# The rests of u chunks 7, 8 and 15 to 24: from GpSimd to VectorE, between its routing operations

## The reference

```python
def peer(xn, w_q, sub_keys, u, v):                 # xn: 256 x 1024
    q = (xt @ w_q).reshape(t, PEER_HEADS, 2, PEER_HALF)
    sc = jnp.einsum("thpc,hpnc->thpn", q, sub_keys).astype(jnp.float32)
    top_s, top_i = lax.top_k(sc, PEER_TOPK)        # 16 of 128 keys, for 8 heads and 2 halves
    cand_s = (top_s[:, :, 0, :, None] + top_s[:, :, 1, None, :]).reshape(...)   # 16 x 16 sums
    best_s, best_pos = lax.top_k(cand_s, PEER_TOPK)
    idx = jnp.take_along_axis(cand_i, best_pos, axis=-1)
    gate = jax.nn.softmax(best_s, axis=-1)
    ...
    act = jnp.einsum("cd,ced->ce", xc, u[ic]).astype(jnp.float32)
    hid = (jax.nn.gelu(act, approximate=False) * gc).astype(xc.dtype)
    return jnp.einsum("ce,ced->cd", hid, v[ic])
```

## Time and profile before

| | |
|---|---|
| three runs, us | 1731.01, 1735.48, 1737.76 |
| their median | 1735.48 us |
| the profiled execution's own time | 1731.88 us |
| its span (first to last instruction) | 1729.9 us |
| busy share of the span | PE 93%, PEld 75%, DVE 74%, ACT 46%, POOL 23% |
| mean granted clock of TensorE | 0.976 of full speed |

### The profile page before, as it was taken

The page is one execution under the profiler, slowest core; times in us unless marked ns, Lnnn a source line. Parts: engine busy times, 40 slices in busy tenths (PEclk is TensorE's granted clock), DMA queues, the critical chain, the costliest instruction groups (busy, mean ns, idle before and its releaser), DMA issues. The chain is left out here.

```text
span 1729.9 us, 24818 instructions
## 1 busy us (share of the span) xinstructions
PE 1610.1 (93%) x9420; PEld 1303.3 (75%) x9420; DVE 1278.4 (74%) x1565; ACT 798.1 (46%) x1033; POOL 392.7 (23%) x184
## 2 busy tenths in 40 slices
PE   7995899899999996999988999999999999999997
PEld 7855555455555553988878999999999988888886
DVE  5244888888778886777626997666777788888886
ACT  4413777777667775456534334666666300000000
POOL 6601211111111110000155889322222100000000
PEclk9996899999999999999999999999999999999999
DMA  8407799999999988433413544444444555555553
GB/s 320 153 1 305 284 422 412 412 416 411 411 360 411 416 363 294 181 134 133 160 50 115 179 170 156 160 147 147 147 147 147 188 190 193 194 194 194 194 194 121
DMA packets 45903, 398.89 MB, mean 231 GB/s; under 512 B 10120, under 2 KB 12424, under 8 KB 13576
## 3 DMA queue, kind: packets, MB, share of 16 engines
q1 hardware_dynamic: 45832, 397.89, 60.4%
HBM read 395.77 MB, written 3.01 MB: 231 GB/s over the span
## 5 line engine op out<-in xcount | busy, mean ns | idle before, releaser
L2124 DVE TENSOR_TENSOR ring_rest<-ring,w_lead 128x2048 fp32r<-128x2048 f32 x128 | 293.4, 2343 | 37.7 <-ACT w_lead L1153 37.7
L1153 ACT ACTIVATE w_lead<-ring 128x2048 fp32r<-128x2048 f32 x128 | 239.5, 1905 | 22.0 <-DVE ring_rest L2124 18.2
L654 ACT ACTIVATE xhat<-h 128x1024 f32<-128x1024 f32 x6 | 6.3, 1054 | 384.7 <-DVE h L2493 349.7
L1597 PE MATMUL bank<-ring_rest,x_two 128*128 128x512 f32 x512 | 140.3, 406 | 32.2 <-DVE ring_rest L2124 32.2
L1315 ACT ACTIVATE lead<-raw 128x2048 fp32r<-128x2048 f32 x64 | 122.3, 1913 | 88.9 <-PE bank L1832 88.7
L1891 PE MATMUL bank<-lead,hid_hi 128*128 128x512 f32 x512 | 157.9, 390 | 0.9 <-DVE hid_lo L2468 0.8
L1891 PE MATMUL bank<-rest,hid_hi 128*128 128x512 f32 x512 | 157.7, 389 | 0.0
L1891 PE MATMUL bank<-lead,hid_lo 128*128 128x512 f32 x512 | 157.6, 389 | 0.0
L1597 PE MATMUL bank<-w_lead,x_two 128*128 128x512 f32 x512 | 146.1, 424 | 11.3 <-POOL x_two L1002 6.6
L1832 PE MATMUL bank<-nT_hi,rest 128*128 128x256 f32 x1024 | 143.9, 283 | 8.9 <-POOL rest L1019 8.9
L1828 PE MATMUL bank<-nT_hi,lead 128*128 128x256 f32 x1024 | 147.7, 287 | 2.6 <-ACT lead L1315 2.6
(11 more groups left out here) (340 smaller groups left out, 2881.3 us busy)
## 6 DMA issues: line engine op xcount, KB each, us to landing
ring<-in_w_gate SPq DMA_DIRECT2D x32, 2048.0 KB, 9.8
ring<-in_w_up SPq DMA_DIRECT2D x32, 2048.0 KB, 10.2
ring<-in_w_down SPq DMA_DIRECT2D x32, 2048.0 KB, 10.5
raw<-in_u SPq DMA_DIRECT2D x64, 1024.0 KB, 4.8
raw<-in_v SPq DMA_DIRECT2D x64, 1024.0 KB, 4.8
ring<-in_w_in SPq DMA_DIRECT2D x14, 2048.0 KB, 10.8
ring<-in_w_out SPq DMA_DIRECT2D x4, 2048.0 KB, 7.9
ring<-in_w_q SPq DMA_DIRECT2D x4, 2048.0 KB, 7.7
```

Of the source, the lines that this page charges most:

```text
L1153: act.activation(w_lead[half][:, :, :], ring8(slot)[:, 4 * half:4 * half + 4, :], ACT.Copy).then_inc(w_lead_ready, 1)
L1597: last = pe.matmul(bank[kind][:, :], x_two[j][:, 4 * half + k, :], part[:, k, :], start=(ready is w_lead_ready and half == 0 and k == 0), ...
L2124: dve.tensor_tensor(ring_rest8(slot)[:, part, :], ring8(slot)[:, part, :], w_lead[half][:, :, :].bitcast(F32), ALU.subtract).then_inc(w_re ...
```

## The change

The same subtraction, on the same buffers, is made for 12 of the first 25 chunks by VectorE. GpSimd makes chunks 0 to 6, waits until the rests of 7 and 8 are made (`rest_ready` at 9), and makes 9 to 14. VectorE waits for `rest_ready` at 7 ahead of the `cand` sums and makes rests 7 and 8, one ahead of each sum; it waits for `rest_ready` at 15 ahead of the four `match` passes and makes two rests in each pass (15 to 22), one before the softmax's sum (23) and one after it (24). The chunks at which the one-hots begin stay where they were (`FIRST_MIXED` is 25 in both). GpSimd's loop of six rests is written out.

```diff
-POOL_RESTS = ROUTING + 1
+VECTOR_EARLY = (7, 8)
+VECTOR_FROM = 15
...
-            with pool.Fori(0, ROUTING // UNROLL) as i:
-                for s in range(UNROLL):
-                    pool_rest(UNROLL * i + s, s)
-            for n in range(ROUTING, POOL_RESTS):
+            for n in range(VECTOR_EARLY[0]):
+                pool_rest(n, n)
+            pool.wait_ge(rest_ready, VECTOR_EARLY[-1] + 1)
+            for n in range(VECTOR_EARLY[-1] + 1, VECTOR_FROM):
                 pool_rest(n, n)
...
+            def rest_of(n):
+                slot, b = n % RAW_SLOTS, n % 2
+                dve.wait_ge(lead_ready, n + 1)
+                dve.tensor_tensor(rest[slot][:, :], raw[slot][:, :], lead[b][:, :].bitcast(F32), ALU.subtract).then_inc(rest_ready, 1)
...
+            dve.wait_ge(rest_ready, VECTOR_EARLY[0])
             for t in range(NT):
+                rest_of(VECTOR_EARLY[t])
                 last = dve.tensor_tensor(cand[:, t, :, :, :], spread(half_of(ts, t, 0).unsqueeze(3), wide),
                                          spread(half_of(ts, t, 1).unsqueeze(2), wide), ALU.add)
...
+            dve.wait_ge(rest_ready, VECTOR_FROM)
             for half in range(2):
                 for t in range(NT):
+                    n = VECTOR_FROM + 2 * (2 * half + t)
+                    rest_of(n)
                     link(dve.tensor_tensor(match[:, :, :], spread(c("iota")[:, 0:TOPK].unsqueeze(1), [P, HK, TOPK]),
                                            spread(bdigf[:, half, t, :].unsqueeze(2), [P, HK, TOPK]), ALU.is_equal))
...
                     link(dve.tensor_tensor(by_head, by_head, spread(half_of(tif, t, half).unsqueeze(2), wide), ALU.mult))
+                    rest_of(n + 1)
                     link(dve.tensor_reduce(ij[:, half, t, :], match[:, :, :], AX_X, ALU.add))
...
             dve.tensor_tensor(by_head, by_head, spread(best_sum[:, :].unsqueeze(2), flat), ALU.subtract).then_inc(routed, 1)
+            for n in range(VECTOR_FROM + 8, ROUTING):
+                rest_of(n)
...
+            rest_of(ROUTING)
             dve.wait_ge(route_turned, 1)
...
-            dve.wait_ge(rest_ready, POOL_RESTS)
-            rest_of(POOL_RESTS)
+            rest_of(FIRST_MIXED)
```

More of the change, by code:

```diff
@@ L105 @@
 HOTS = 3
-FIRST_MIXED = POOL_RESTS
+FIRST_MIXED = ROUTING + 1
 LAST_MIXED = PEER_CHUNKS - 2
@@ L2407, in _ @@
             dve.tensor_copy(ijT[:, 1, :], bank[ROUTE_BANK[1]][:, 0:T]).then_inc(route_ready, 1)
[L2410 to L2413, removed]
             def one_hots(g):
```

## The result

| | before | changed |
|---|---|---|
| median, us | 1735.48 (7 runs, 1731.01 to 1738.04) | 1723.29 (7 runs, 1721.41 to 1726.23) |
| profiled execution's own time, us | 1731.88 | 1723.27 |
| its span, us | 1729.9 | 1721.4 |

The ratio is 0.9936 with a 95% interval of 0.992 to 0.9953: faster by 0.64%, between 8 and 14 us.

What follows compares the result with a forecast made beforehand. GpSimd and VectorE, taking turns, were taken to set the pace in the match passes and stall TensorE; 2.26 us at chunks 7 and 8 plus 8.23 at 14 to 21 gave 10.5 less, 1724 us, range 1717 to 1731.

Steps and rivals of the forecast that it cites:

- What bounds it: TensorE in the routing: late rests lose 2.26 us at chunks 7 and 8 and 8.23 at 14 to 21.
- Turns: GpSimd's rests and VectorE's swollen operations don't overlap; a match pass needs 13.2 us of both, TensorE only 11.4.
- The price of 2.29 for the multiplication: Match passes: the multiplication, 6.56 us beside GpSimd's rests, was taken at 2.29 once GpSimd is out of the way.
- The margins: Match passes of 11.4 to 11.6 us; rest 16 ready 1.3 us before TensorE asks, odd chunks' rests over 2.
- The cast `tif`: Ahead of the `cand` sums on VectorE: the cast would end at 972.68 us as before, having waited for rest 6.
- The claim that nothing behind the routing gives time back: Past the routing every engine runs as before, 10.5 us earlier; TensorE's `v` waits for VectorE come to 0.8 us.
- The sum: Whole kernel: 10.5 us less, giving 1721.4 from the profiled execution, 1725.0 from the median, 1723.5 from the mean; stated 1724.
- B: Match passes longer than 11.6 us; at 12.9 a pass 4.6 us are given back, 1728.5; chance 0.08.
- C: Loads can't hold the pace, or GpSimd's margin at chunks 9 and 14 fails: 2 us given back, 1726; chance 0.08.
- D: Match passes: the long rows are the operations' own time, a pass needs 17.7 us; slower by 13.4, 1747; chance 0.03.
- E: Match passes: the two engines bound each other as before, pace stays 6.6 us; no gain, 1734; chance 0.03.
- The caution about moving work from one engine of this pair to the other: Twelve rests from GpSimd to VectorE: by the skill's shared read port warning the sum would be 0, by the rows 10.5.

Runs made afterwards that it cites:

- pair_last: Changed kernel with both rests of a pass behind its three match operations; ratio to before 0.9985, stretch 138.23 us against the changed kernel's 131.28.
- pair_first: Changed kernel with both rests of a pass ahead of its three match operations; ratio to before 0.9958, stretch 133.92 us.
- after_again: The unchanged text of the changed kernel, run once more; ratio to before 0.9949, stretch 131.26 us.
- dummy_read: Changed kernel with nine subtractions added on idle GpSimd, behind the leads of chunks 15 to 23, results unread; ratio to before 1.0075, stretch 154.67 us.
- late_only: Changed kernel with rests 7 and 8 given back to GpSimd, so only 15 to 24 are on VectorE; ratio to before 0.9959, stretch 133.52 us.
- rest0_vector: Changed kernel with the rest of chunk 0 made by VectorE too, in its second search; ratio to before 0.9937, stretch 131.27 us.

## Why the prediction was right

- **What bounds it.** The loss read from the chunks' starts, 2.26 + 8.23 us, is what the two halves of the change gave back, 2.26 and 8.22. Reading it from the idle time alone would have given 8.9 less chunk 0's wait, so 7.9 us for both. The missing 2.6 us are 0.26 us at each of the ten waits: in chunk 14 the eight lead matmuls before the wait start at 1019.54, and such a group takes 0.94 us to the next; the rest matmuls start at 1022.22, so 1.74 us late where the row says 1.57 idle; and it is 1.05 us from them to the next group in place of 0.95.
- **Turns.** That GpSimd's rests and VectorE's operations wait for one another was argued from starts and ends. The one-input passes and the added reads now show it from both sides: put reductions in place of VectorE's two-input operations, and GpSimd's rests shrink to 4.63; give GpSimd something to read, and VectorE's operations grow.
- **The price of 2.29 for the multiplication** was the most open term (up to 6.56; with the comparison at 4.26 too, that would have meant 1747). It came out at 2.29, four times.
- **The margins.** Rest 15 started 2.83 us after the start of chunk 14 (2.7 expected), a pass took 11.38 to 11.42 us (11.4 to 11.6), and no rest was late. `pair_last` and `pair_first` show that this was the working part: the same operations in another order lose 2.6 or 7 of the 10.5 us.
- **What was off.** The cast `tif` didn't wait for rest 6: it started at 968.18, 1 us ahead of that rest, and took 0.43. `bdig` waited 3.83 us, not 3.1. TensorE and GpSimd were 1.4 us later at chunk 6 than in the profile before, through chunk 0, and VectorE was not, which accounts for both. Neither moved anything, but the room differs: VectorE idled 6.29 us ahead of rest 7, and only 0.33 us ahead of rest 15. The claim that nothing behind the routing gives time back was off by 0.6 us: TensorE's waits for VectorE in the `v` part were 1.4 us, not 0.8.
- **The sum.** 10.5 us forecast and 10.46 measured in the stretch; 1724 forecast and 1723.29 measured. Against the profiled execution alone the sum gave 1721.4, where 1723.27 came: the missing 1.9 are chunk 0's 1.5 and some tenths. For the same reason the last span came out at 1721.4 and not at the 1719 to 1720 given as a sign. That the medians hit 1724 within 1 us is partly luck: they lie 12.2 us apart in this comparison and 8.0 in that of `after_again`, with the same 10.5 us in the stretch both times.
- **Rivals.** B, C, D and E are refuted by the full stretch: no late rest, no wait for a load, operations at 2.29, no leftover of the old pace. The caution about moving work from one engine of this pair to the other was not borne out as a sum of 0, and holds in another way: the gain came from keeping GpSimd from reading beside VectorE's two-input operations, and the version that moves six more rests away from harmless places loses it again.

## What to carry to other kernels

Where two engines' operations swell beside each other, first sort the operations by what they read, and check it in the rows: here GpSimd's subtractions cost nothing beside VectorE's searches and reductions, and 2 to 4 us each beside its large two-input operations, but a cast, a shift and a copy of one input waited as well. Move only those that collide, and put each one ahead of the moment at which it is asked for, counted in operations from the trace. Take TensorE's loss from the starts of its chunks, not from its idle rows, which here left out a quarter of it.

## What the runs showed of the hardware that was not expected

- A fill on GpSimd, which reads nothing, left the 128x2048 comparison and multiplication at 2.28 and 2.29 us but held a 128x16 copy for 1.90 us in place of 0.17.
- What one wait costs TensorE depends on its length. After the waits of 0.2 to 1.6 us in chunks 1 to 23 the granted clock was 1.00. After 4.11 and 7.48 us it was 0.86 and 0.84 in the 12 us that followed, and 0.83 and 0.81 after the 8.53 and 7.35 us of `dummy_read`: the first 24 matmuls took 4.46 to 5.02 us in place of 2.85, so 1.6 to 2.2 us more were lost.
- Chunk 0 comes in two forms, whatever the kernel. It follows a wait of 2.58 us. In the kernel before, in `late_only` and in `rest0_vector` its first eight matmuls already ran at the lower clock (2.05 us for eight) and it took 8.46, 8.45 and 7.07 us; in the other nine profiles they ran at full clock (1.18 or 1.19 us) and the lower clock came later, within the second eight and over the first rest matmuls (2.07 or 2.08 us for eight), with 9.95 to 10.03 us for the chunk. The waits for its rest were longer there too, 1.71 to 1.87 us, to 0.99 and 1.12. What decides between them was not found; without the edit of `rest0_vector` it moves a time by 1.5 us, a seventh of this change's gain.
